# Four weight buffers parked in two row slots while the expert rows start, and another order of selection, queries and rows

## The chip, the cores and the metric

One core of a Trainium2 chip runs the whole kernel in one launch. Times are microseconds of device time; the metric is the median of the runs.

## The reference, cut to what matters

Two blocks of two layers each work on 256 tokens of 1024 features in fp32. The second block is the one that the change touches. A layer of it mixes four token mixers, projects, and then routes every token to expert rows:

```
q  = (x @ w_q)                       # 8 heads, 2 halves of 128 each
sc = q . sub_keys                    # 128 scores for each half
top 16 of each half -> 256 sums -> best 16, idx; gate = softmax(best)
act = gelu(u_tab[idx] . x)           # 16384 rows of 1024 in each table
y  += (gate * act) * v_tab[idx]      # 8 heads x 16 rows for each token
```

## The kernel before, in words

**Weights** come as a stream of chunks of 128 x 1024 fp32 (0.524 MB). SP loads chunk c into a raw buffer. ScalarE writes its high part (L1369), GpSimd (L1247) or VectorE (L2069) the low part, raw minus high; TensorE multiplies with both and adds to w_used when a chunk is used. A raw buffer is free when the low part is made, so SP waits for the low part of the buffer's chunk before. The second block has 42 chunks a layer: 18 for the mixers' input, 8 for the output projection (18 to 25), and 26 to 41 are the query weights, two for each of the 8 heads. It uses four raw buffers. The split chunks lie in w_split, six pairs; pairs 4 and 5 serve chunks 22 and 23 only, the later query chunks take pairs 0 and 1.

**Rows.** The 256 tokens are two tiles of 128. With 8 heads and 16 picks, a layer fetches 256 gathers (called rows in the code, ROWS), each one row of the joined table (2048 fp32) for each of 128 tokens, 1.049 MB. GpSimd issues them as indirect DMAs (L1331) into slots. VectorE takes the dot products of the first half of the row with x (L2419), ScalarE applies gelu and the gate and makes diagonal matrices (L1692 to L1703), TensorE multiplies these with the second half of the row and accumulates over the tile (weighted_rows). They go in batches of two; a unit is one head of one tile, 16 gathers or 8 batches. Ten slots are used up to gather 89, fifteen from 90 on. Slots 6 to 9 lie over w_split: 6 and 7 over pairs 4 and 5, 8 and 9 over pairs 2 and 3.

**Order.** Each engine works off a queue written out by hand. Gathers start while the queries of the later heads are still to be computed. VectorE picks the experts of a unit in six parts (stages), put behind dots of batches by SELECT_AT. TensorE's halves of a query and its key scores stand between batches (QUERY_AT, QUERY_LATER); GpSimd's low parts of the query chunks stand between gathers (LOWS_AT). GpSimd waits before a gather for its slot: for w_used where weights lay there, else for row_used of the slot's gather before. Since its queue has one order, whatever stands behind such a wait waits too. At a layer's end SP resets semaphores (turn) and loads the next layer's first three chunks.

## Time and profile before

| | us |
|---|---|
| median of 3 runs | 2305.95 (2296.69 to 2306.26) |
| the profiled execution's own time | 2299.8 |
| its span | 2297.7 |
| TensorE, VectorE, GpSimd, ScalarE busy | 1951.7, 1401.6, 1190.8, 950.0 |
| gathers, all 512: share of 16 DMA engines | 56.4% |

The span is that of the instructions on the one core; the execution's own time has 2.1 us more around it. The two layers of the first block end at 680, the two of the second block take 680 to 1490 and 1490 to 2298. A busy share is a mean over stages with different limits, so the stages are read one by one. Clock times in the text are us from the span's start.

### The profile page before, as it was taken

The numbers are of one execution on the slowest core, as the hardware profiler recorded it, in microseconds if no ns is written. First come the engines' busy times: TensorE is split into PE (matmuls) and PEld (weight loads), VectorE is DVE, ScalarE is ACT, GpSimd is POOL, SyncE is SP. The second block draws the span as 40 slices with busy tenths as digits, with TensorE's granted clock in tenths as the row PEclk, the third lists the DMA queues.
The fourth block names the chain that finished last, engine by engine and source line by source line (L and its number), as shares of the span: only waits on it lengthen the run. The fifth ranks groups of instructions, "written<-read, shape, count | busy, mean of one in ns | idle before, by whom it ended". The sixth has DMA issues, their size and how long they took to land.

```text
span 2297.7 us, 26964 instructions
## 1 busy us (share of the span) xinstructions
PE 1951.7 (85%) x8576; PEld 1287.0 (56%) x8576; DVE 1401.6 (61%) x3166; ACT 950.0 (41%) x2289; POOL 1190.8 (52%) x816
## 2 busy tenths in 40 slices
PE   7989998999999889987777777798899877777776
PEld 6889998789988765543223222387654422232222
DVE  6442116531127888776777665578897767776655
ACT  6644336644335534333233332356344332333322
POOL 6759868758873156645344343141466544443441
PEclk9999999999999989999999999998899999999999
DMA  5436544435545289999999999763799999999997
GB/s 180 148 114 201 184 159 161 157 112 191 183 172 210 92 327 403 421 420 421 421 421 420 422 420 421 292 221 108 294 415 421 420 421 421 421 421 422 421 421 293
DMA packets 118020, 700.27 MB, mean 305 GB/s; under 512 B 13968, under 2 KB 13968, under 8 KB 51856
## 3 DMA queue, kind: packets, MB, share of 16 engines
q0 software_dynamic: 73728, 536.90, 56.4%
q1 hardware_dynamic: 44176, 161.96, 20.3%
q8 instruction: 56, 0.92, 0.2%
q14 instruction: 60, 0.49, 0.1%
HBM read 697.76 MB, written 1.05 MB: 304 GB/s over the span
## 4 chain that ended last, share of the span: by engine, by line
PE 46%; DMA 38%; DVE 7%; ACT 4%; issue 3%; POOL 2%; DVEq 0%; SPq 0%; POOLq 0%; ACTq 0%
PE ps L648 45%; DMA late_row<-in_table,arena 18%; DMA arena<-in_table,arena 16%; DMA row_sb<-in_table,arena 3%; DVE late_row L2419 1%; POOL w_split L1247 1%; POOL arena L1331 1%; DVE arena L2419 1%; DVE arena L2083 1%; ACT diag L1703 1%; DVE w_split L2069 1%; POOL late_row L1331 1%; ACT w_split L1369 0%; ACT arena L1697 0%; ACT arena L1692 0%
## 5 line engine op out<-in xcount | busy, mean ns | idle before, releaser
L1247 POOL TENSOR_TENSOR w_split<-raw,w_split 128x1024 fp32r<-128x1024 f32 x248 | 606.0, 2468 | 329.1 <-ACT w_split L1369 326.6
L648 PE MATMUL ps<-late_row,diag 128*128 128x512 f32 x1000 | 467.6, 610 | 129.4 <-ACT diag L1703 129.4
L648 PE MATMUL ps<-hT_hi,w_split 128*128 128x256 f32 (+1 forms) x2688 | 522.3, 292 | 14.2 <-DVE hT_lo L2145 5.3
L648 PE MATMUL ps<-arena,diag 128*128 128x512 f32 x888 | 424.8, 620 | 124.3 <-ACT diag L1703 124.3
L648 PEld LDWEIGHTS ps<-hT_hi,w_split 128*128 128x128 f32 x2688 | 435.8, 196 | 26.2 <-issue 13.8
L1331 POOL DMA_INDIRECT late_row<-in_table,arena x250 | 266.5, 1066 | 322.3 <-PE ps L648 294.8
L2419 DVE CUSTOM_DVE_ANT_0 late_row<-late_row,x_res 128x1024 f32<-128x1024 f32 x250 | 317.7, 1274 | 170.1 <-DMA late_row<-in_table,arena 164.4
L1331 POOL DMA_INDIRECT arena<-in_table,arena x222 | 247.2, 1113 | 325.7 <-PE ps L648 265.6
L648 PEld LDWEIGHTS ps<-late_row,diag 128*128 128x128 f32 x1000 | 183.0, 192 | 401.7 <-ACT diag L1703 216.6
L648 PE MATMUL ps<-hT_lo,w_split 128*128 128x256 f32 (+2 forms) x1344 | 386.8, 288 | 0.0
L2419 DVE CUSTOM_DVE_ANT_0 arena<-arena,x_res 128x1024 f32<-128x1024 f32 x222 | 289.0, 1306 | 154.4 <-DMA arena<-in_table,arena 150.3
L1692 ACT ACTIVATE arena<-arena 128x2 f32<-128x2 f32 x260 | 52.6, 202 | 766.0 <-DVE arena L2419 765.7
L648 PEld LDWEIGHTS ps<-arena,diag 128*128 128x128 f32 x888 | 163.9, 194 | 363.7 <-ACT diag L1703 199.3
L1369 ACT ACTIVATE w_split<-raw 128x1024 fp32r<-128x1024 f32 x288 | 300.7, 1059 | 160.9 <-DMA raw<-in_stream 112.5
L648 PEld LDWEIGHTS ps<-hT_lo,w_split 128*128 128x128 f32 (+1 forms) x1344 | 263.9, 196 | 7.7 <-issue 5.7
L648 PE MATMUL ps<-w_split,hT_hi 128*128 128x512 f32 x640 | 204.9, 402 | 15.5 <-DVE arena L1936 3.6
L1834 DVE TENSOR_TENSOR arena<-arena,ps 128x256 f32<-128x256 f32 x44 | 18.5, 421 | 303.0 <-ACT arena L1419 303.0
L1703 ACT ACTIVATE diag<-ident,arena 128x128 f32<-128x128 f32 x512 | 174.2, 387 | 0.3
L648 PEld LDWEIGHTS ps<-w_split,hT_hi 128*128 128x128 f32 x640 | 120.4, 192 | 47.0 <-issue 9.1
L1697 ACT ACTIVATE arena<-arena 128x1 f32<-128x1 f32 x512 | 123.3, 287 | 8.5
L648 PE MATMUL ps<-w_split,hT_lo 128*128 128x512 f32 x320 | 126.7, 396 | 0.0
L648 PE MATMUL ps<-w_split,hidw_hi 128*128 128x512 f32 x352 | 109.4, 392 | 0.0
(280 smaller groups left out, 1940.1 us busy)
## 6 DMA issues: line engine op xcount, KB each, us to landing
raw<-in_stream SPq DMA_DIRECT2D x288, 512.0 KB, 3.3
row_sb<-in_row SPq DMA_DIRECT2D x2, 2306.5 KB, 10.7
late_row<-in_table,arena POOLq DMA_INDIRECT x250, 30.2
arena<-in_table,arena POOLq DMA_INDIRECT x222, 29.3
arena<-in_sub SPq DMA_DIRECT2D x2, 1024.0 KB, 10.4
arena<-in_small SPq DMA_DIRECT2D x2, 640.0 KB, 8.4
x_res<-in_x SPq DMA_DIRECT2D x1, 1024.0 KB, 5.8
out_x<-x_res SPq DMA_DIRECT2D x2, 512.0 KB, 5.2
```

The costliest lines, as they stand in the source:

```text
L648: ins = nc.tensor.matmul(o, lhsT, rhs, start=start, stop=stop)
L1247: pool.tensor_tensor(w_lo[pair], raw[:, at % raws, :], w_hi[pair].bitcast(F32), ALU.subtract).then_inc(lo_ready, 1)
L1331: pool.indirect_dma_start(out=slots[slot_of[n]], out_offset=None, in_=table, in_offset=bass.IndirectOffsetOnAxis(ap=picked[:, u, at:at + 1 ...
L1369: A(w_hi[pair_of(c, self.pairs, self.narrow)], raw[:, slot, :], ACT.Copy).then_inc(hi_ready, 1)
L1692: A(acts[:, some], dots[:, some], ACT.Gelu).then_inc(acts_ready, 1)
L1697: A(acts[:, n:n + 1], acts[:, n:n + 1], ACT.Copy, scale=gate[:, n // TOP, n % TOP:n % TOP + 1]).then_inc(acts_gated, 1)
L1703: A(diag[:, n % DIAGS, :], ident[:], ACT.Copy, scale=acts[:, n:n + 1]).then_inc(diag_ready, 1)
L1834: V.tensor_tensor(full, value, gate, ALU.mult).then_inc(gate_step, 1)
L2069: V.tensor_tensor(w_lo[pair], raw[:, c % RAW2, :], w_hi[pair].bitcast(F32), ALU.subtract).then_inc(dve_lo_ready, 1)
L2083: step(V.scalar_tensor_tensor(out=dst[:, c, :], in0=x, scalar=tap, in1=dst[:, c, :], op0=ALU.mult, op1=ALU.add))
L2419: ins = V.tensor_tensor_reduce(out=x, in0=x, in1=x_res[:, n // TILE_ROWS, :], scale=1.0, scalar=0.0, op0=ALU.mult, op1=ALU.add, accum_out= ...
```

## The change

The second block gets nine raw buffers. Five are used in turn for all chunks but four; the fifth of them is the memory of three constant tiles (rel, after, before), which the second block doesn't need once its masks are made. The other four, the parked ones, are the halves of row slots 6 and 7 and hold the query chunks 30 to 33, loaded when 24 chunks are used. Gathers 0 to 11 run on the eight other slots (FIRST_LAP); gather 12 is the first in slot 6 and 15 the first in slot 7, each after the low parts of the chunks parked there. From 16 to 89 the ten slots are used in turn, then fifteen.

The queues at the opening change: TensorE takes key scores 1 before the first batch, and puts the halves of query 2 behind batches 0 and 1. ScalarE empties query 1 before the first diagonals and query 2 before those of batch 2. GpSimd makes the low parts of head 2 before gathers 10 and 11, of head 3 before 12 and 14, of head 4 before 16 and 20. Heads 5 to 7 stay at the first and fifth gather of a unit. Selection of unit u ends behind batch 8u - 7 instead of some batches earlier, and the gates' exponential moves with it. At the end of a layer that another follows, SP waits for all dots before it loads the next layer's first chunks.

```diff
@@ -49,7 +49,8 @@
...
-RAW2, PAIR2 = 4, 4
+RAW2, PAIR2, PARKED = 5, 4, 4
+PARAMS_AT, LATE_AT = 3, 5
@@ -75,13 +76,19 @@
...
-LOWS_AT = {14: (2, 0), 15: (2, 1), 17: (3, 0), 19: (3, 1), 24: (4, 0), 28: (4, 1)}
-LOWS_AT.update({(h - HEADS_FIRST) * TOP + 4 * k: (h, k) for h in range(5, PH) for k in range(2)})
-QUERY_AT = {0: (5, 6, 7), 1: (2, 4, 6)}
-QUERY_LATER = (0, 2, 5)
-OPENING = 3
+LOWS_AT = (10, 11)
+HEAD_LOWS_AT = (12, 14)
+OPENING = 2
+RAW_HOME = ([c % RAW2 for c in range(N2_NARROW)] + [RAW2 + k for k in range(PARKED)]
+            + [c % RAW2 for c in range(N2_NARROW, N2 - PARKED)])
+NTH_RAW = [RAW_HOME[:c].count(RAW_HOME[c]) for c in range(N2)]
+RAW_BEFORE = [max((k for k in range(c) if RAW_HOME[k] == RAW_HOME[c]), default=None) for c in range(N2)]
+PARK_FREE = N2_MIX + 6
+FIRST_LAP = (0, 1, 2, 3, 4, 5, 8, 9, 0, 1, 2, 3, 6, 4, 5, 7)
+LAP = (8, 9, 0, 1, 2, 3, 6, 4, 5, 7)
...
-SELECT_AT = {0: 0, 1: 0, 2: 3, 3: 3, 4: 0, 5: 2}
+SELECT_AT = {0: 0, 1: 2, 2: 2, 3: 2}
+SELECT_AT.update({b: 1 for u in range(2, UNITS) for b in range(u * UNIT_BATCHES - 12 + (u == 2), u * UNIT_BATCHES - 6 + (u == 2))})
@@ -186,14 +193,14 @@
...
+        MASKS = 3 + 3 * AH + 4
...
-        raw = sb("raw", [P, max(RAW1, RAW2), CH])
+        raw = sb("raw", [P, RAW2 - 1, CH])
...
-        rel = sb("rel", [P, 3 * P])
-        after = sb("after", [P, 3 * P])
-        before = sb("before", [P, 3 * P])
+        distances = sb("distances", [P, 3, 3 * P])
+        rel, after, before = distances[:, 0], distances[:, 1], distances[:, 2]
@@ -229,6 +236,8 @@
...
+        raws_at = [raw[:, k, :] for k in range(RAW2 - 1)] + [distances.rearrange("p k c -> p (k c)")[:, 0:CH]]
+        raws_at += [late_row[:, 2 + k // 2, k % 2 * CH:(k % 2 + 1) * CH] for k in range(PARKED)]
@@ -368,8 +377,10 @@
...
-        assert ALL_SLOTS_FROM % QUERY_SLOTS == 0
-        slot_of = [n % QUERY_SLOTS if n < ALL_SLOTS_FROM else (n - ALL_SLOTS_FROM + QUERY_SLOTS) % SLOTS for n in range(ROWS)]
+        turned = (ALL_SLOTS_FROM - len(FIRST_LAP)) % len(LAP)
+        FULL_LAP = (*range(QUERY_SLOTS, SLOTS), *LAP[turned:], *LAP[:turned])
+        slot_of = [FIRST_LAP[n] if n < len(FIRST_LAP) else LAP[(n - len(FIRST_LAP)) % len(LAP)] if n < ALL_SLOTS_FROM
+                   else FULL_LAP[(n - ALL_SLOTS_FROM) % SLOTS] for n in range(ROWS)]
@@ -539,7 +550,7 @@
...
-                sp.dma_start(raw[:, slot, :], stream[c]).then_inc(w_ready[slot], 16)
+                sp.dma_start(raws_at[slot], stream[c]).then_inc(w_ready[slot], 16)
@@ -562,20 +573,26 @@
...
                 for c in range(EARLY, N2):
-                    if c >= RAW2:
-                        low_part_made(sp, c - RAW2)
-                    load(base + c, c % RAW2)
+                    if RAW_BEFORE[c] is not None:
+                        low_part_made(sp, RAW_BEFORE[c])
+                    if RAW_HOME[c] == RAW2:
+                        sp.wait_ge(w_used, PARK_FREE)
                     if c == RAW2 - 1:
+                        sp.wait_ge(mask_ready, MASKS)
+                    load(base + c, RAW_HOME[c])
+                    if c == PARAMS_AT:
                         for dst, src in params:
                             sp.dma_start(dst, src).then_inc(par_ready, 16)
-                    if c == RAW2 + N2 % RAW2 - 1:
+                    if c == LATE_AT:
                         for dst, src in late:
...
 
-            def turn(n, chunks, low, following):
+            def turn(n, chunks, low, following, rows=0):
 
...
                 sp.wait_ge(lo_ready, low)
+                if rows and following is not None:
+                    sp.wait_ge(dots_ready, rows)
                 sp.sem_inc(first, 1)
@@ -609,7 +626,7 @@
...
                         store_tile(t)
-                turn(l + (1 + DEPTH), N2, low_parts(N2 - 1), following)
+                turn(l + (1 + DEPTH), N2, low_parts(N2 - 1), following, BATCHES)
 
@@ -1166,26 +1182,24 @@
...
                 query(1, 1)
+                key_scores(1)
                 weighted_rows(0)
-                key_scores(1)
+                query(2, 0)
                 weighted_rows(1)
-                weighted_rows(2)
-                query(2, 0)
-                weighted_rows(3)
                 query(2, 1)
-                key_scores(2)
-
-
-                for b in range(OPENING + 1, BATCHES):
+
+
+                for b in range(OPENING, BATCHES):
                     u, at = BATCH_ROWS[b][0] // TOP, BATCH_ROWS[b][0] % TOP // BATCH
...
                     h = u + HEADS_FIRST
-                    first_half, second_half, scored_at = QUERY_AT.get(u, QUERY_LATER)
-                    if h < PH and at == first_half:
+                    if b == OPENING:
+                        key_scores(HEADS_FIRST - 1)
+                    if h < PH and at == (2 if u == 0 else 0):
                         query(h, 0)
-                    if h < PH and at == second_half:
+                    if h < PH and at == (4 if u == 0 else 2):
                         query(h, 1)
-                    if h < PH and at == scored_at:
+                    if h < PH and at == (6 if u == 0 else 5):
                         key_scores(h)
@@ -1311,17 +1325,22 @@
...
                     u, at = n // TOP, n % TOP
+                    h = u + HEADS_FIRST
+                    if h < PH and at == (HEAD_LOWS_AT[0] if u == 0 else 0):
+                        query_low_part(h, 0)
+                    if h < PH and at == (HEAD_LOWS_AT[1] if u == 0 else 4):
+                        query_low_part(h, 1)
                     if n in LOWS_AT:
-                        query_low_part(*LOWS_AT[n])
+                        query_low_part(HEADS_FIRST - 1, LOWS_AT.index(n))
                     if u == 0 and at in FIRST_PICKS:
...
                         pool.wait_ge(picks_ready, u + len(FIRST_PICKS))
-                    if n == FREE_SLOTS - 2:
-                        pool.wait_ge(w_used, N2_QUERY - 2)
-                    if n == FREE_SLOTS:
+                    if n == FIRST_LAP.index(8):
 
                         pool.wait_ge(w_used, N2_NARROW - 2)
+                    if n in (FIRST_LAP.index(6), FIRST_LAP.index(7)):
+                        low_part_made(pool, N2_NARROW + (1 if slot_of[n] == 6 else 3))
                     if n == ALL_SLOTS_FROM:
@@ -1362,11 +1381,13 @@
...
-                    slot = c % self.raws
-                    act.wait_ge(w_ready[slot], i * (16 * step // self.raws) + 16 * (c // self.raws + 1))
+                    in_block2 = self.narrow == N2_NARROW
+                    slot = RAW_HOME[c] if in_block2 else c % self.raws
+                    nth = NTH_RAW[c] if in_block2 else c // self.raws
+                    act.wait_ge(w_ready[slot], i * (16 * step // self.raws) + 16 * (nth + 1))
...
-                    A(w_hi[pair_of(c, self.pairs, self.narrow)], raw[:, slot, :], ACT.Copy).then_inc(hi_ready, 1)
+                    A(w_hi[pair_of(c, self.pairs, self.narrow)], raws_at[slot], ACT.Copy).then_inc(hi_ready, 1)
@@ -1703,34 +1724,30 @@
...
                 query_high_part(2, 0)
+                empty_query(1)
                 diags_of(0)
-                empty_query(1)
+                empty_scores(1)
+                query_high_part(2, 1)
                 diags_of(1)
-                empty_scores(1)
-                diags_of(2)
-                query_high_part(2, 1)
-                diags_of(3)
                 query_high_part(3, 0)
                 empty_query(2)
+                diags_of(2)
+                empty_scores(2)
                 query_high_part(3, 1)
-                empty_scores(2)
                 for b in range(OPENING + 1, BATCHES):
...
                         gate_exp(1)
-                    if b == UNIT_BATCHES:
-                        gate_exp(2)
-                    first_half, second_half, scored_at = QUERY_AT.get(u, QUERY_LATER)
-                    if h + 1 < PH and at == (2 if u > 1 else first_half + 1):
+                    if h + 1 < PH and at == (4 if u == 0 else 2):
                         query_high_part(h + 1, 0)
-                    if h < PH and at == (4 if u > 1 else second_half + (u == 1)):
+                    if h < PH and at == (5 if u == 0 else 4):
                         empty_query(h)
-                    if h + 1 < PH and at == (5 if u > 1 else second_half + 1):
+                    if h + 1 < PH and at == (6 if u == 0 else 5):
                         query_high_part(h + 1, 1)
-                    if 0 < u < UNITS - 2 and at == 6:
-                        gate_exp(u + 2)
+                    if 0 < u < UNITS - 1 and at == 3:
+                        gate_exp(u + 1)
                     if h < PH and at == 7:
@@ -2469,7 +2486,7 @@
...
                     dots_of(b)
-                    for _ in range(SELECT_AT.get(b, 1 if b < 2 * UNIT_BATCHES or 1 <= at <= len(stages) else 0)):
+                    for _ in range(SELECT_AT.get(b, 0)):
                         if picking:
```

Left out are the same changes of names at each use of the buffers (raws_at, RAW_HOME) and of rel, after and before.

## Rows read from the trace of the kernel before

**Rows 1.** The page: its span, the chunk's high part, the chunk loads.

```profile
span 2297.7 us, 26964 instructions
...
L1369 ACT ACTIVATE w_split<-raw 128x1024 fp32r<-128x1024 f32 x288 | 300.7, 1059 | 160.9 <-DMA raw<-in_stream 112.5
...
raw<-in_stream SPq DMA_DIRECT2D x288, 512.0 KB, 3.3
```

**Rows 2.** Windows: length, busy PE, PEld, DVE, ACT, POOL, granted clock, DMA share, GB/s.

```profile
800.00:810.00 10.00, 8.22 (x70) 7.57 (x67) 8.34 (x21) 3.14 (x9) 0.00 (x0) 1.00 0.01 2
810.00:820.00 10.00, 8.69 (x48) 8.72 (x48) 9.48 (x31) 2.33 (x3) 3.67 (x3) 0.64 0.40 132
820.00:830.00 10.00, 9.28 (x54) 8.91 (x53) 6.20 (x18) 5.11 (x9) 7.73 (x8) 0.67 1.01 418
...
890.00:900.00 10.00, 9.47 (x35) 5.27 (x35) 8.99 (x19) 3.43 (x15) 8.60 (x7) 1.00 0.91 336
```

**Rows 3.** The same view, 100 us of the steady stretch.

```profile
1150.00:1250.00 100.00, 75.23 (x158) 29.88 (x159) 72.31 (x167) 36.78 (x115) 43.54 (x40) 0.97 1.01 421
```

**Rows 4.** The same view, the second layer's opening.

```profile
1710.00:1720.00 10.00, 10.00 (x42) 5.94 (x41) 8.00 (x13) 4.23 (x14) 8.44 (x5) 1.00 1.01 397
```

**Rows 5.** SP's queue in order of time: start us, us, what, how many.

```profile
795.38 0.33 SPq L542 DMA_DIRECT2D raw<-in_stream  x1
...
818.04 1.46 SPq L542 DMA_DIRECT2D raw<-in_stream  x2
...
842.27 0.33 SPq L542 DMA_DIRECT2D raw<-in_stream  x1
...
915.62 0.33 SPq L542 DMA_DIRECT2D raw<-in_stream  x1
...
990.00 1.28 SPq L542 DMA_DIRECT2D raw<-in_stream  x3
```

**Rows 6.** The chain that ended last, at the first layer's end: start us, us, what.

```profile
1480.78 1.23 DVE late_row L2419
...
1490.53 1.28 ACT L1369
```

**Rows 7.** ScalarE in order of time, early in the mixing stage.

```profile
701.86 1.06 ACT L1369 ACTIVATE w_split<-raw 128x1024 fp32r<-128x1024 f32 x1 [1.25 <-DMA raw<-in_stream]
```

**Rows 8.** GpSimd in order of time: start us, us, engine, line.

```profile
810.86 1.13 POOL L1331 DMA_INDIRECT arena<-in_table,arena  x1 [15.50 <-DVE arena L2348]
...
832.88 0.94 POOL L1331 DMA_INDIRECT arena<-in_table,arena  x1 [3.01 <-PE ps L648]
...
839.89 2.36 POOL L1247 TENSOR_TENSOR w_split<-raw,w_split 128x1024 fp32r<-128x1024 f32 x1
...
852.58 1.67 POOL L1331 DMA_INDIRECT late_row<-in_table,arena  x1 [4.87 <-DVE arena L2397]
```

**Rows 9.** TensorE in order of time, the same columns.

```profile
830.62 3.70 PE L648 MATMUL ps<-arena,diag 128*128 128x512 f32 x8 [0.78 <-ACT diag L1703]
834.16 1.05 PE L648 MATMUL ps<-arena 128*128 128x128 f32 x8
...
842.39 0.36 PE L648 MATMUL ps<-hT_hi,w_split 128*128 128x256 f32 x1
...
845.22 0.28 PE L648 MATMUL ps<-hT_hi,w_split 128*128 128x256 f32 x1
849.13 5.40 PE L648 MATMUL ps<-late_row,diag 128*128 128x512 f32 x8 [3.63 <-ACT diag L1703]
```

**Rows 10.** ScalarE in order of time, the opening.

```profile
828.27 1.28 ACT L1692 ACT_TABLE_LOAD   x1
...
830.19 0.68 ACT L1703 ACTIVATE diag<-ident,arena 128x128 f32<-128x128 f32 x2
830.77 0.57 ACT L1664 ACTIVATE arena<-ps 128x512 f32<-128x512 f32 x1
```

**Rows 11.** TensorE in order of time, the second layer's opening.

```profile
1657.90 3.70 PE L648 MATMUL ps<-late_row,diag 128*128 128x512 f32 x8 [3.63 <-ACT diag L1703]
```

More of the change, by code:

```diff
@@ L426, in two_blocks_kernel @@
         arrived = {n: sem(f"{n}_arrived") for n in ("pe", "act", "dve", "pool")}
-        w_ready = [sem(f"w_ready{i}") for i in range(max(RAW1, RAW2))]
+        w_ready = [sem(f"w_ready{i}") for i in range(RAW2 + PARKED)]
         first = sem("layer_first")
@@ L620, in two_blocks_kernel @@
         CONSTS = 4
-        MASKS = 3 + 3 * AH + 4
         LAST_SUMS = 2 + 2 * TT + TT
@@ L1202, in _ @@
             pool.memset(ident[:], 0.0).then_inc(const_ready, 1)
-            pool.iota(rel[:], pattern=[[1, 3 * P]], base=-P, channel_multiplier=-1,
+            pool.iota(rel, pattern=[[1, 3 * P]], base=-P, channel_multiplier=-1,
                       allow_small_or_imprecise_dtypes=True).then_inc(rel_ready, 1)
@@ L1219, in second_constants @@
                 for h in range(AH):
-                    pool.tensor_scalar(window[:, h], rel[:], 2.0 ** (-2.0 * (h + 1)) * 64 ** 0.5, 0.0, ALU.mult,
+                    pool.tensor_scalar(window[:, h], rel, 2.0 ** (-2.0 * (h + 1)) * 64 ** 0.5, 0.0, ALU.mult,
                                        ALU.add).then_inc(mask_ready, 1)
@@ L1246, in low_part @@
                 pair = pair_of(at, pairs, narrow)
-                pool.tensor_tensor(w_lo[pair], raw[:, at % raws, :], w_hi[pair].bitcast(F32),
+                pool.tensor_tensor(w_lo[pair], raws_at[RAW_HOME[at] if narrow == N2_NARROW else at % raws], w_hi[pair].bitcast(F32),
                                    ALU.subtract).then_inc(lo_ready, 1)
@@ L1760, in setup @@
                 dve.wait_ge(rel_ready, 1)
-                step(V.tensor_scalar(after[:], rel[:], 0.0, None, ALU.max))
-                step(V.tensor_scalar(before[:], rel[:], -1.0, 0.0, ALU.mult, ALU.max))
+                step(V.tensor_scalar(after, rel, 0.0, None, ALU.max))
+                step(V.tensor_scalar(before, rel, -1.0, 0.0, ALU.mult, ALU.max))
                 step.settle()
-                step(V.tensor_tensor(absd[:], after[:], before[:], ALU.add))
+                step(V.tensor_tensor(absd[:], after, before, ALU.add))
                 step.settle()
@@ L2068, in low_part @@
                         dve.wait_ge(w_used, used_before(c, PAIR2, N2_NARROW))
-                    V.tensor_tensor(w_lo[pair], raw[:, c % RAW2, :], w_hi[pair].bitcast(F32),
+                    V.tensor_tensor(w_lo[pair], raws_at[RAW_HOME[c]], w_hi[pair].bitcast(F32),
                                     ALU.subtract).then_inc(dve_lo_ready, 1)
```

## The prediction

> **What bounds the kernel now.** I read four views, in this order. The page gives the span, 2297.7 us, and the forms of the weight work [rows 1]. Then the windows, because the question of this change is who supplies the DMA engines. In each of the two layers of the second block the reader should see three states: before the expert rows start the engines are nearly idle (2 GB/s at 800 to 810), from about 820 they run at 418, and from then on at 421 until the rows are through [rows 2, 3]. A gather is 128 x 8 KB = 1.049 MB, so at 421 GB/s it costs 2.49 us of DMA time, and 256 of them 638 us. That is the whole time from 820 to the last landing at 1480.8 but for what else passes through the same engines. TensorE is idle a quarter of it. So a layer of the second block is (start of the gathers) + (bytes still to move) / 421 + (DMA idle time), and nothing that happens on an engine counts unless it changes one of the three. Third, the queues of SP, GpSimd, TensorE and ScalarE at the opening, for the order in which they release each other. Last, the chain of waits at the layer's end.
>
> The exact start of the full stretch: 810 to 820 moved 1.32 MB, of which 1.05 is gather 0; the other 0.27 MB is 0.65 us, so 819.35 [rows 2]. Idle time in the present opening: 336 instead of 421 GB/s in 890 to 900 is 2.0 us, and with the small deficits of the other windows about 2.6. The second layer's only large one is 397 GB/s over 10 us, 0.6; call it 0.9 in all [rows 4].
>
> **Bytes taken out of the full stretch.** Now chunk c waits for the low part of c - 4, so SP's issues can be numbered backwards: 31 at 795.4, 32 and 33 at 818.0, and eight (34 to 41) from 842.3 to 915.6 [rows 5]. Ten chunks of 0.524 MB pass while the engines are full, 1.245 us each. After the change 30 to 33 have buffers of their own and wait only until 24 chunks are used, which is inside the output projection, shortly before 800; behind them in SP's queue 34 waits for the low part of 25, 35 and 36 for those of 26 and 27 (the latter is what released SP at 795.4). All are ready. So 30 to 36, 3.7 MB or 8.7 us, go at about 797 into a stretch that moved 2 GB/s. 37 and 38 wait for 28 and 29, as 32 and 33 do now, and go at 818; 39 to 41 later. Five chunks remain instead of ten: **-6.2 us a layer, -12.5 in all**.
>
> **The next layer's first loads.** They are issued at 990.0, three chunks amid full DMA [rows 5]. The new wait on all dots moves them to about 1482.1, when the DMA is idle: **-3.7 us**, once. SP has nothing queued behind them but the layer's turn. They are covered by the last sums and the norm: a chunk lands 3.3 us after issue [rows 1], 1485.4, and ScalarE begins the next layer at 1490.5 [rows 6]. Without that cover they would cost those 3.3 us. The last layer has no such loads.
>
> **Fifth buffer in the mixing stage.** ScalarE waited 1.25 us for a chunk at 701.9, on the path [rows 7]; I found no other such wait on the chain. It can be worth 0 to 1.25 us a layer; I take **-1** for both. The wait on the masks is met before the layer opens. The five parts of selection that move to later batches lie on VectorE, which waits for rows; the last part of unit u runs behind the dots of batch 8u - 7, its first row needs slot space from batch 8u - 5 on ten slots. Nothing.
>
> **The opening, where the cost is.** Gathers 0 to 7 are issued as now, from 810.9 on [rows 8]. Then today gathers 8 and 9 have slots too, 10 to 13 follow the first two batches of weighted rows, and no query stands between these batches; gather 16 goes at 852.6. After the change gather 8 needs gather 0's slot, and the queues interlock: the low part of head 2 stands in GpSimd's queue in front of gather 10, and the first half of query 2 stands in TensorE's in front of batch 1, which frees gather 10's slot. I walk it with durations of the rows: a batch 3.7 us, its first gather's slot handed to GpSimd 2.26 after its start (830.62 to 832.88), half a query 3.1 (842.4 to 845.5), key scores 1.05, low part 2.4, emptying a bank 0.6, high part 1.06, a table load 1.28, from its end to the first diagonal 1.07 [rows 1, 8 to 10].
> - Query 1 ends at 829.84 (0.78 before 830.62). ScalarE empties it first, 830.45, then loads the table and makes the diagonals, 832.8. Batch 0 starts 2.2 later than now: gathers 8 and 9 at 835.1 and 836.9.
> - Low part (2,0) 837.9 to 840.3; half query to 843.5; batch 1; gather 10 at 845.8. Low part (2,1) to 849.4; gather 11 at 849.6.
> - Half query (2,1) to 852.6, and low part (3,0) before gather 12, 853.9. ScalarE has emptying query 2 in front of batch 2's diagonals: 854.3; gather 13 at 856.5, batch 2 ends 858.0.
> - Key scores 2 to 859.05, emptied 859.65, high part (3,1) 860.7, low part 863.2: gather 14 at 863.3, 15 at 865.3.
> - Gather 16 stands behind low part (4,0), whose high part ScalarE makes after batch 4's diagonals. These come after batch 3's (1.5), the gate's exponential (a table load and 0.4) and a second table load: 866.6; high part 867.6, low part 870.1, **gather 16 at 870.2** against 852.6 now.
>
> Its data flow from about 871.5 (an issue takes 1.1 to 1.8 on GpSimd [rows 8]). Between 819.35 and 871.5 the DMA then has gathers 1 to 15 (37.4 us) and chunks 37 and 38 (2.5): 39.9 of 52.1 us. **12.2 us idle a layer**, 24.4 in all, for the present 2.6 + 0.9: **+20.9**. From gather 17 on GpSimd issues faster than 2.49 us again and ten slots are enough, as now.
>
> TensorE's clock: after 3.6 us of waiting the batch at 849.1 took 5.4 us, not 3.7; the same batch of the second layer, after the same wait, took 3.7 [rows 9, 11]; and the window at 810 to 820 had a mean granted clock of 0.64, between the two levels of 1.2 and 2.4 GHz [rows 2]. The new opening has a wait of 3.9 us (836.5 to 840.4) and several of 2. With three waits to meet it I take one such slowdown a layer, 1.7: **+3.4**.
>
> **Sum.** -12.5 - 3.7 - 1 + 20.9 + 3.4 = **+7**. Against the profiled execution's own 2299.8 that is 2307; that execution is 6 below the median of 2306 (2297 to 2306). I forecast **2313 us**. About 0.5%, 11.5 us, is what a measurement can tell from no change.
>
> **Rivals.**
> 1. The supply holds, faster. Place: gathers 8 to 16. If queries and batches overlapped better than my walk, only the two missing slots would count, 5 us of DMA time a layer: 10 - 3.5 - 12.5 - 3.7 - 1 = -11, 2295. For it: landing times in full stretches leave some gathers queued. Against: each step of the walk is a wait in a queue with one order. It decides if gather 16 goes before about 863; at 10 us idle a layer the change is even.
> 2. TensorE falls to the lower clock for most of the opening, slower. Two half queries and three batches on the walk's path at 1.5 to 1.7 more each are 8 us a layer, where I took 1.7: 13 more, 2326. For it: the slow batch above came after one such wait and the opening makes three. Against: in the steady stretch, with TensorE idle a quarter of the time in short pieces, the clock was 0.97 [rows 3]. The Trainium skill, TensorE: Matmul & The Clock Gate (Part 1: The HAM clock gate), says that throttled is the default state and only activity releases it; by that rule each long wait starts the next piece slow, which is this rival; the trace shows it for one such wait of two.
> 3. The change does not take bytes out, because PARK_FREE or the order in SP's queue holds the parked loads until 818: the 6.2 a layer are gone, 2325. The window at 800 to 810 speaks against it.
> 4. The moved first loads are not covered: +3.3, inside the range.
>
> **Chances.** The walk as it stands (2303 to 2321) 0.50; rival 1 0.20; rival 2 0.22; rival 3 and the rest 0.08. The range from rival 1 to rival 2 is 2295 to 2328. Of the first case about a seventh lies above 2317.5, and a small part of rival 1 within 0.5%: faster 0.17, same 0.48, slower 0.35.
>
> **What would show it.** SP's seven issues at about 797 and a DMA share near 0.9 at 797 to 806; two issues at 818; no load at 990 but three at 1482. Gather 8 at 835, gather 10 at 846, gather 14 at 863, gather 16 at 870; DMA windows well below 421 between 845 and 871, none below after 880. GpSimd's wait before gather 10 ended by TensorE, TensorE's before query 2 by GpSimd. The prediction is wrong if the windows from 845 to 870 stay near 421, or if the stream after 880 shows new gaps.

## The result, and the profile after

The changed kernel took 2317.15 us (median of 7 runs, 2311.73 to 2320.37), the kernel before 2303.98 on the same chip (7 runs, 2296.69 to 2306.26). The ratio is 1.0055, interval 1.0041 to 1.0068: slower by 13 us. The forecast was 2313, which was +7 on the median of 2306 that the kernel before then had. The profiled execution of the changed kernel took 2317.15 as well, with a span of 2315.2; that of the kernel before (2299.8) lies below its median, so between the two traces the spans differ by 17.5 us.

**What came as forecast.** SP's queue in order of time, in the first layer's opening (start us, us, what, how many). It answers to [rows 5]:

```profile
800.06 1.75 SPq L553 DMA_DIRECT2D late_row<-in_stream  x4
801.85 1.46 SPq L553 DMA_DIRECT2D raw<-in_stream  x3
...
820.31 0.33 SPq L553 DMA_DIRECT2D raw<-in_stream  x1
821.45 0.33 SPq L553 DMA_DIRECT2D distances<-in_stream  x1
...
1489.66 1.28 SPq L553 DMA_DIRECT2D raw<-in_stream  x3
```

The four parked chunks go into the row slots, three more into raw buffers behind them, all seven between 800.06 and 803.4; two more follow once the first gathers are out, and nothing goes at 990, for the next layer's first loads now stand at the layer's end. The whole trace is 2.3 us late here (gather 0 at 813.13 in the place of 810.86) because the first block took so much longer in this execution; that stretch moves by chance (below), so what follows counts from gather 0.

Windows of the first opening (length, busy PE, PEld, DVE, ACT, POOL, granted clock, DMA share, GB/s). They answer to [rows 2]:

```profile
800.00:810.00 10.00, 8.93 (x70) 8.25 (x68) 8.94 (x18) 1.94 (x5) 0.00 (x0) 1.00 0.90 339
...
830.00:840.00 10.00, 8.12 (x34) 4.88 (x32) 6.41 (x23) 6.26 (x15) 0.81 (x1) 0.83 1.02 425
840.00:850.00 10.00, 5.53 (x28) 4.80 (x27) 9.40 (x23) 0.00 (x0) 4.17 (x3) 0.83 0.72 280
850.00:860.00 10.00, 7.66 (x32) 5.43 (x30) 5.59 (x9) 1.10 (x2) 8.06 (x5) 0.83 0.60 206
860.00:870.00 10.00, 8.49 (x43) 5.96 (x44) 4.26 (x13) 5.53 (x14) 3.86 (x3) 1.00 0.64 215
870.00:880.00 10.00, 9.55 (x40) 5.63 (x39) 5.41 (x15) 5.67 (x17) 7.95 (x7) 1.00 0.71 265
880.00:890.00 10.00, 10.00 (x30) 4.88 (x29) 8.96 (x21) 5.08 (x18) 8.11 (x7) 1.00 1.01 419
```

The engines that moved 2 GB/s at 800 to 810 now move 339, and the price is the hole from 840 to 880: 280, 206, 215, 265. The same four windows of the kernel before had nearly the full stream:

```profile
840.00:850.00 10.00, 6.37 (x33) 4.23 (x32) 9.61 (x23) 1.35 (x6) 7.36 (x4) 1.00 1.01 417
850.00:860.00 10.00, 8.52 (x39) 5.52 (x37) 8.94 (x13) 2.93 (x4) 6.00 (x3) 0.83 1.02 421
860.00:870.00 10.00, 8.79 (x20) 4.13 (x21) 9.46 (x30) 6.83 (x20) 4.96 (x3) 0.83 1.02 419
870.00:880.00 10.00, 8.92 (x54) 6.79 (x53) 9.64 (x20) 2.08 (x5) 6.75 (x6) 1.00 1.01 415
```

As idle DMA time I count each 5 us window's missing share of 421 GB/s, from 15 to 130 us after gather 0; windows above 421 count against it. It is 17.1 us in the first layer and 14.6 in the second. The kernel before had 2.6 and 0.9.

**Why the hole is there.** GpSimd in order of time (start us, us, engine, line, what, idle before and its releaser). It answers to [rows 8]:

```profile
839.20 0.94 POOL L1350 DMA_INDIRECT arena<-in_table,arena  x1 [10.37 <-PE ps L664]
840.79 1.68 POOL L1350 DMA_INDIRECT arena<-in_table,arena  x1 [0.66 <-PE ps L664]
842.49 2.36 POOL L1261 TENSOR_TENSOR w_split<-late_row,w_split 128x1024 fp32r<-128x1024 f32 x1
851.59 1.14 POOL L1350 DMA_INDIRECT arena<-in_table,arena  x1 [6.74 <-PE ps L664]
852.75 2.50 POOL L1261 TENSOR_TENSOR w_split<-late_row,w_split 128x1024 fp32r<-128x1024 f32 x1
855.40 0.96 POOL L1350 DMA_INDIRECT arena<-in_table,arena  x1 [0.15 <-issue]
856.38 2.38 POOL L1261 TENSOR_TENSOR w_split<-late_row,w_split 128x1024 fp32r<-128x1024 f32 x1
858.92 1.76 POOL L1350 DMA_INDIRECT late_row<-in_table,arena  x1 [0.16 <-POOL w_split L1261]
863.77 0.94 POOL L1350 DMA_INDIRECT arena<-in_table,arena  x1 [3.09 <-PE ps L664]
867.76 2.38 POOL L1261 TENSOR_TENSOR w_split<-late_row,w_split 128x1024 fp32r<-128x1024 f32 x1 [3.06 <-ACT w_split L1390]
870.28 1.76 POOL L1350 DMA_INDIRECT row_sb<-in_table,arena  x1
...
876.62 0.95 POOL L1350 DMA_INDIRECT late_row<-in_table,arena  x1
```

and TensorE, the same columns, which answers to [rows 9]:

```profile
835.12 5.40 PE L664 MATMUL ps<-arena,diag 128*128 128x512 f32 x8 [1.10 <-ACT diag L1724]
844.99 0.35 PE L664 MATMUL ps<-hT_hi,w_split 128*128 128x256 f32 x1 [4.47 <-POOL w_split L1261]
...
849.30 0.29 PE L664 MATMUL ps<-hT_hi,w_split 128*128 128x256 f32 x1
849.43 3.60 PE L664 MATMUL ps<-arena,diag 128*128 128x512 f32 x8
855.30 0.39 PE L664 MATMUL ps<-hT_hi,w_split 128*128 128x256 f32 x1 [2.27 <-POOL w_split L1261]
```

Read the two together, by the names behind the arrows. Gather 8 waited 10.37 us for TensorE's batch 0. Only behind gathers 8 and 9 does GpSimd take off the low part of query (2,0), at 842.49. TensorE waited 4.47 us for that low part, worked half a query, and then batch 1. Gather 10 waited 6.74 us for batch 1. It is the interlock of the prediction, link by link, with both engines waiting in turn: TensorE has 5.53 of 10 us in the window from 840. Against the walk, counted from gather 0:

| us after gather 0 | gather 8 | 10 | 12 | 13 | 14 | 16 |
|---|---|---|---|---|---|---|
| predicted | 24.2 | 34.9 | 43.0 | 45.6 | 52.4 | 59.3 |
| first layer | 26.1 | 38.5 | 45.8 | 50.6 | 57.1 | 63.5 |
| second layer | 23.2 | 35.3 | 43.1 | 47.7 | 54.2 | 60.5 |

In the kernel before gather 8 went at 16.0, 10 at 22.0, 14 at 31.5 and 16 at 41.7.

### The profile page after: what moved, and what is told of

It is laid out like the page before. It is cut to its first block, busy times and chain, and to the rows that moved or that the text cites. A ratio compares the mean times of both kernels' runs of the same rounds, so it can differ in the third digit from the quotient of the medians.

```text
span 2315.2 us, 27031 instructions
## 1 busy us (share of the span) xinstructions
PE 1958.5 (85%) x8576; PEld 1292.2 (56%) x8576; DVE 1394.4 (60%) x3166; ACT 947.1 (41%) x2287; POOL 1196.2 (52%) x816
## 4 chain that ended last, share of the span: by engine, by line
PE 46%; DMA 38%; DVE 6%; ACT 4%; POOL 4%; issue 4%; DVEq 0%; ACTq 0%; POOLq 0%; SPq 0%
PE ps L664 44%; DMA arena<-in_table,arena 21%; DMA late_row<-in_table,arena 16%; POOL w_split L1261 2%; DMA row_sb<-in_table,arena 1%; POOL arena L1350 1%; DVE arena L2436 1%; DVE arena L2100 1%; DVE late_row L2436 1%; DVE w_split L2086 1%; ACT diag L1724 1%; POOL late_row L1350 0%; ACT w_split L1390 0%; PE ps L696 0%; ACT hT_hi L1413 0%
## 5 line engine op out<-in xcount | busy, mean ns | idle before, releaser
L1261 POOL TENSOR_TENSOR w_split<-raw,w_split 128x1024 fp32r<-128x1024 f32 x236 | 577.2, 2470 | 328.6 <-ACT w_split L1390 328.0
L2436 DVE CUSTOM_DVE_ANT_0 late_row<-late_row,x_res 128x1024 f32<-128x1024 f32 x246 | 310.2, 1263 | 180.1 <-DMA late_row<-in_table,arena 174.1
L1390 ACT ACTIVATE w_split<-raw 128x1024 fp32r<-128x1024 f32 x266 | 278.2, 1058 | 122.0 <-DMA raw<-in_stream 112.4
L664 PE MATMUL ps<-row_sb,diag 128*128 128x512 f32 x160 | 81.4, 633 | 33.9 <-ACT diag L1724 33.9
```

Of the source, the lines that this page charges most:

```text
L664: ins = nc.tensor.matmul(o, lhsT, rhs, start=start, stop=stop)
L1261: pool.tensor_tensor(w_lo[pair], raws_at[RAW_HOME[at] if narrow == N2_NARROW else at % raws], w_hi[pair].bitcast(F32), ALU.subtract).then_ ...
L1390: A(w_hi[pair_of(c, self.pairs, self.narrow)], raws_at[slot], ACT.Copy).then_inc(hi_ready, 1)
L2436: ins = V.tensor_tensor_reduce(out=x, in0=x, in1=x_res[:, n // TILE_ROWS, :], scale=1.0, scalar=0.0, op0=ALU.mult, op1=ALU.add, accum_out= ...
```

## The experiments

All ratios are to the kernel before, with runs of it on the same chip; the intervals are of 95%. The plain quotient of the two medians differs from the ratio by up to 0.0012 (2.8 us). "Idle" is the DMA idle time of the two openings, summed as above; the kernel before has 3.5 us in both together, the changed one 31.7.

**The moved first loads, taken back.** The changed kernel without the turn's wait for the dots:

```
-turn(l + (1 + DEPTH), N2, low_parts(N2 - 1), following, BATCHES)
+turn(l + (1 + DEPTH), N2, low_parts(N2 - 1), following)
```

> The changed kernel, but SP does not wait for the dots before it loads the next layer's first three chunks. Theory (the opening's queues starve the DMA, the moved loads are a gain): the three loads go back to about 993, amid full DMA, the first layer's rows end 3.7 us later, time about 4 us above the changed kernel, 2320 to 2322 (ratio to the kernel before 1.007). Rival (the moved loads are not covered at the layer's turn and are part of the loss): time 3 us below the changed kernel, 2314.

Measured: 2320.7 us, ratio 1.0071 (1.0054 to 1.0089), 0.0016 or 3.7 us above the changed kernel's, the size of the term; but the two intervals overlap.

**The buffers with the order of before.** The changed kernel's nine buffers and moved loads, with before's order of queries, batches and selection; the low parts of head 2 stand at rows 10 and 12, since the parked slots must be emptied:

```
-LOWS_AT = (10, 11)
-OPENING = 2
+LOWS_AT = {10: (2, 0), 12: (2, 1), 17: (3, 0), ...}
+OPENING = 3
...
-FIRST_LAP = (0, 1, 2, 3, 4, 5, 8, 9, 0, 1, 2, 3, 6, 4, 5, 7)
+FIRST_LAP = (0, 1, 2, 3, 4, 5, 8, 9, 0, 1, 2, 3, 6, 4, 5, 8, 9, 0, 1, 7)
```

> The changed kernel's nine buffers and its moved loads, with the order of queries, batches, empties and selection of the kernel before; the low parts of head 2 stand before gathers 10 and 12, slot 6 starts with gather 12, slot 7 with gather 19. Theory (the interlock of low part, query and batch is the loss, not the buffers): idle DMA time at the opening falls from 17 and 15 us to 2 to 5 a layer, gather 16 is issued about 853 to 857, time 2291 to 2297 (ratio 0.995 to 0.997). Rival (two slots fewer are the loss, whatever the order): idle stays at 10 or more a layer, time 2305 or above.

Measured: 2300.52 us, 0.9983 (0.9968 to 0.9998), idle 11.7. The loss is gone while the buffers stay, so it lies in the new order (of queries, batches, low parts and selection taken together); a small gain over before is left, smaller than expected.

**Eight slots alone.** Before, with rows on eight slots until row 12 and nothing else:

```
-slot_of = [n % QUERY_SLOTS if n < ALL_SLOTS_FROM else ...]
+FIRST_LAP = (0, 1, 2, 3, 4, 5, 8, 9, 0, 1, 2, 3, 6, 4, 5, 7)
```

> The kernel before, whose gathers use slots 6 and 7 only from gathers 12 and 15 on, in the changed kernel's order of slots; nothing else is changed. Theory: gathers 8 to 11 follow the first two batches as their slots come free, the DMA stays fed, at most 2 us a layer, ratio 1.000 to 1.002. Rival (the missing slots are the loss): 5 us or more a layer, ratio 1.004 or above.

Measured: 0.9996 (0.9982 to 1.0011), idle 3.9. Gather 8 goes at 23.1 in the place of 16.0, gather 12 at 29.9 in the place of 26.4, and the stream shows no hole: the eight gathers already issued are 20 us of data. Two slots fewer cost nothing that the times show.

**The moved loads alone.** Before, with the turn's new wait.

> The kernel before with one part of the change alone: SP waits for all dots before the next layer's first three loads. Theory: 3.7 us less, ratio 0.998 to 0.999, loads landed before ScalarE asks for them. Rival (not covered): ratio 1.000 to 1.002, with ScalarE's first high part of the next layer waiting for a DMA.

Measured: 0.9988 (0.9974 to 1.0003). Both the expected -3.7 us and no change at all lie inside the interval, so it decides nothing.

**The low parts of head 2 sooner.** The changed kernel with one line edited:

```
-LOWS_AT = (10, 11)
+LOWS_AT = (8, 9)
```

> The changed kernel with the low parts of head 2 in front of gathers 8 and 9 instead of 10 and 11; nothing else. Theory (the interlock): the half queries 2 no longer wait for GpSimd, batches 1 and 2 start 4 to 6 us earlier, gather 16 is issued about 56 us after gather 0 instead of 60.5 to 63.5, idle falls by 4 to 6 us a layer, time 8 to 12 below the changed kernel: 2305 to 2310, ratio 1.000 to 1.003. Rival (two slots fewer, or the clock, is the loss and the position of two subtractions is not): 2315 to 2319.

Measured: 2290.57 us, 0.9936 (0.9912 to 0.9961), from 4 runs; idle 11.6; gather 16 at 51.8. The direction was right and the size far more than expected. The profiled execution is the slowest of the four (2299.63), 9 us above their median, so its trace can show only a part of that size. GpSimd and TensorE of this kernel:

```profile
831.17 2.93 POOL L1261 TENSOR_TENSOR w_split<-late_row,w_split 128x1024 fp32r<-128x1024 f32 x1 [1.97 <-ACT w_split L1390]
838.45 0.95 POOL L1350 DMA_INDIRECT arena<-in_table,arena  x1 [4.34 <-PE ps L664]
839.42 2.40 POOL L1261 TENSOR_TENSOR w_split<-late_row,w_split 128x1024 fp32r<-128x1024 f32 x1
841.98 0.96 POOL L1350 DMA_INDIRECT arena<-in_table,arena  x1 [0.16 <-issue]
844.25 1.29 POOL L1350 DMA_INDIRECT arena<-in_table,arena  x1 [1.31 <-PE ps L664]
```

```profile
835.69 3.70 PE L664 MATMUL ps<-arena,diag 128*128 128x512 f32 x8 [1.10 <-ACT diag L1724]
838.83 0.68 PE L664 MATMUL ps<-hT_hi,w_split 128*128 128x256 f32 x1
...
842.10 3.60 PE L664 MATMUL ps<-arena,diag 128*128 128x512 f32 x8
845.13 0.68 PE L664 MATMUL ps<-hT_hi,w_split 128*128 128x256 f32 x1
```

The first subtraction now lies in the 10 us in which GpSimd waited for batch 0 anyway. TensorE goes from batch 0 to the half query to batch 1 with no wait between them, and from 830 on its granted clock is 1.00: half a query takes 3.3 us (838.83 to the batch at 842.10), not 4.4. The windows:

```profile
840.00:850.00 10.00, 8.56 (x51) 6.44 (x50) 9.47 (x17) 2.43 (x7) 7.93 (x6) 1.00 1.02 420
850.00:860.00 10.00, 9.86 (x46) 6.53 (x47) 9.79 (x16) 5.54 (x13) 5.12 (x4) 1.00 0.77 307
860.00:870.00 10.00, 9.55 (x40) 5.64 (x39) 9.69 (x27) 5.66 (x19) 8.68 (x6) 1.00 0.83 297
```

**Batch 1 ahead of query (2,0).** In the changed kernel, on TensorE:

```
-query(2, 0)
 weighted_rows(1)
+query(2, 0)
```

> The changed kernel with batch 1 in front of both halves of query 2 on TensorE; nothing else. Theory (all later links of the chain bind until gather 16): gathers 10 and 11 go some 5 us sooner, but batch 2 still stands behind query 2, so gather 16 and with it the idle sum change by at most 2 us a layer: ratio 1.003 to 1.006. Rival (the loss is the late freeing of the slots of gathers 10 and 11): idle falls by 5 us or more a layer, ratio 1.001 or below.

Measured: 0.9983 (0.9969 to 0.9998), idle 20.1, gather 16 at 55.4. My expectation failed and the rival held. Turning two queue entries on TensorE breaks the ring as well: gather 10 goes at 31.9 (38.5 in the changed kernel), gather 11 at 35.5 (42.3), and the later links do not take it back.

**The new selection plan alone.** In the order of before, with the new places of the gates' exponentials that go with it:

```
-SELECT_AT = {0: 0, 1: 0, 2: 3, 3: 3, 4: 0, 5: 2}
+SELECT_AT = {0: 0, 1: 2, 2: 2, 3: 2}
+SELECT_AT.update({b: 1 for u in range(2, UNITS) for b in range(...)})
```

> The kernel before with the changed plan of selection and of the gates' exponentials alone. Theory: no cost and no gain, ratio 0.999 to 1.001, DMA windows after the opening stay at 421. Rival (selection by need comes too late for a unit's first gathers): GpSimd waits on VectorE before the first gather of the units, gaps below 421 in the stream, ratio 1.002 or above.

Measured: 2308.44 us, 1.0022 (1.0008 to 1.0036): about 5 us slower (3 by the medians), idle 8.4, gather 14 at 37.1 after gather 0 (31.5 before). The prediction had put this part at nothing. Its own rival, that GpSimd waits for VectorE at the first gather of a unit, is not what happened: GpSimd waits for TensorE at gather 14, and the idle time of the opening is the whole loss. VectorE and GpSimd of this kernel:

```profile
832.46 0.49 DVE L2305 MAX8 arena<-arena 128x8 f32<-128x128 f32 x2 [1.84 <-ACT arena L1669]
...
837.08 3.35 DVE L2418 CUSTOM_DVE_ANT_0 row_sb<-row_sb,x_res 128x1024 f32<-128x1024 f32 x1
```

```profile
836.65 2.71 POOL L1248 TENSOR_TENSOR w_split<-raw,w_split 128x1024 fp32r<-128x1024 f32 x1
845.59 1.21 POOL L1332 DMA_INDIRECT arena<-in_table,arena  x1 [6.24 <-PE ps L649]
```

The two stages behind batch 1 stand in VectorE's queue ahead of the dots of batch 2, and they wait for ScalarE to empty key scores 1. The second dot of batch 2 so begins 2.9 us later after gather 0 than before (28.6 for 25.7), and it takes 3.35 us in the place of 1.22, as GpSimd subtracts at that moment: 5.0 us together. In the second layer the wait for the key scores is 4.41 us and gather 14 is 7 us late.

**Two parked chunks.** The order of before and the moved loads, with chunks 30 and 31 parked in slot 6 only, so that rows have nine slots until row 12:

```
-RAW2, PAIR2, PARKED = 5, 4, 4
+RAW2, PAIR2, PARKED = 5, 4, 2
```

> The order of the kernel before and the moved loads, five buffers and only chunks 30 and 31 parked, in slot 6; slot 7 takes rows from the start, so nine slots until gather 12. Theory: three chunks leave the full stretch instead of five (-3.7 us a layer), idle falls from the 5 and 7 of the run with four parked to 1 to 3, time 2292 to 2297, at or a little below that run. Rival (the bytes moved out are what counts, the ninth slot not): 3 to 5 us above that run.

Measured: 2293.35 us, 0.9951 (0.9934 to 0.9969), idle 6.9, 7 us below the same order with four parked, which ran on another chip; the intervals just overlap. The row stages of the two are alike (table below), so these 7 us are in no part that the edit explains.

**One low part sooner.** The changed kernel with `LOWS_AT = (8, 11)`.

> Both subtractions of the third head ahead of gathers 8 and 9 made the changed kernel 27 us faster, against the 8 to 12 that I had set down. This one puts only the first of them ahead of gather 8 and leaves the second ahead of gather 11, to see which link of the chain the time hung on. Theory: TensorE gets its half query right behind batch 0 at the full clock (batch 0 and batch 1 at 3.6 to 3.7 us, no half query at 4.6), gathers 8 to 10 go as in the run with both sooner (24.8, 28.3 less the 2.5 us subtraction, and about 30 us after gather 0), and the second subtraction holds the second half query back by some 4 us, so that gather 16 goes at 55 to 56 us after gather 0 (51.8 with both, 63.5 and 60.5 with none) and the idle DMA time is 8 to 10 us a layer (5.8 with both, 17.1 and 14.6 with none): ratio to the kernel before 0.996 to 0.998, so the first subtraction carries some two thirds of the 27 us. Rival: the second one carries as much, since TensorE stands idle ahead of the second half query and works it and the batch behind it at half clock (4.6 and 5.4 us): gather 16 at 58 us or later and a ratio of 1.000 to 1.003.

Measured: 2304.98 us, 1.0009 (0.9996 to 1.0021), idle 16.8, gather 16 at 53.8. The gathers and the idle time are those of the theory (gather 16 even somewhat sooner), the ratio is the rival's; its row stages are 1.6 us shorter than before's, and its mixing stages, 131.7 and 133.1 us, the longest of all. GpSimd of this kernel (gathers 10, 11 and 12 are its gathers here):

```profile
847.82 0.94 POOL L1350 DMA_INDIRECT arena<-in_table,arena  x1 [3.61 <-PE ps L664]
848.78 2.35 POOL L1261 TENSOR_TENSOR w_split<-late_row,w_split 128x1024 fp32r<-128x1024 f32 x1
851.29 0.96 POOL L1350 DMA_INDIRECT arena<-in_table,arena  x1 [0.16 <-issue]
852.27 2.73 POOL L1261 TENSOR_TENSOR w_split<-late_row,w_split 128x1024 fp32r<-128x1024 f32 x1
855.15 1.76 POOL L1350 DMA_INDIRECT late_row<-in_table,arena  x1 [0.15 <-POOL w_split L1261]
```

The first low part gave back about half of the idle time (31.7 to 16.8) and 15.4 of the 19.4 us that both gave in the row stages. The first two batches take 3.7 and 3.6 us, and the second half query, after a wait of 1.92 us, runs at the full clock, so the rival had the ratio but not its reason. The second low part still holds gathers 11 and 12 back while GpSimd works two subtractions with only gather 11 between them.

**Three variants of the run with both low parts sooner.** Nine slots (`PARKED = 2`); the second low part of head 3 ahead of gather 15 (`HEAD_LOWS_AT = (12, 15)`, 14 before); and before's selection plan (SELECT_AT and its default turned back; the gates' exponentials keep their new places).

> The run with both subtractions sooner, with five raw buffers and only chunks 30 and 31 parked (nine row slots until row 12). Theory of the prediction: two chunks a layer go back into the stretch in which the DMA is full, 1.25 us each, +5 us over both layers, and the idle time falls from 5.8 us a layer to about 3, -6 us: within 2 us of the run with both sooner, ratio 0.993 to 0.994. Rival: as between the two runs in the order of before (four parked 0.9983, two parked 0.9951), the ninth slot is worth 7 us more than the bytes cost: ratio near 0.990. Second rival: idle is bound by TensorE's chain, not by slots, and stays at 5 us a layer, so the bytes cost their 5 us: ratio 0.996.

> The run with both subtractions sooner, with the second subtraction of the fourth head ahead of gather 15 in the place of gather 14 (gather 15 needs it anyway, for it takes the slot of the parked chunk). In the run with both sooner gather 14 waited behind it until 858.92, while its own slot had been free since about 854. Theory: gather 14 goes 4 to 5 us sooner (at 40 us after gather 0 in the place of 45), the idle time falls by 2 to 3 us a layer and the ratio by 0.002, to 0.991 to 0.992. Rival: gather 14 takes DMA time that the gathers behind it lack in any case, or the subtraction itself comes 1 us later for it and the half query too: ratio as before, 0.9935 to 0.995.

> The run with both subtractions sooner, with the selection spread of the kernel before (0, 0, 3, 3, 0, 2 stages in the first batches and one in most later ones) and the new places of the gates' exponentials. In the order of before the new spread cost 5 us (ratio 1.0022), with gather 14 at 37 to 39 us after gather 0 against 31.5. Theory: the new spread holds VectorE with two stages in batches 1 to 3 just where rows are waited for, whatever the order of the queries, so taking it back gives 3 to 5 us: ratio 0.991 to 0.992. Rival: in the new order batches 1 and 2 wait for half queries anyway, so the stages stand beside idle time: ratio as with both sooner, 0.9935 to 0.995, or worse where the three stages in batches 2 and 3 hold the dot products.

Measured: 0.9968 (0.9955 to 0.9981), 0.9967 (0.9954 to 0.9979) and 0.9969 (0.9955 to 0.9983), 12 runs each; idle 10.4, 12.2 and 15.0. None beat the run that they started from. In the second, gather 14 went at 40.4 in the place of 45.2, and gather 16 at 51.6 against 51.8, so the data behind it came no sooner: the rival. In the third, gather 8 is 1.4 us later and the next ones up to 2.3. The plan of before gives no gain in this order, although it was the better one in its own. In the changed kernel's trace the two stages wait only 0.46 us for the key scores, which TensorE there computes ahead of batch 0, and batch 2 stands behind both half queries anyway.

**All of them in one table.** "Whole" is the measured ratio as us. "Rows" is read from the profiled executions: from gather 0 to the first table load of the next layer, plus from the second layer's gather 0 to the end, against the 679.7 + 678.1 us of before. The last column is worked out: the idle time over before's 3.5, less 6.2 us a layer for the chunks out of the full stream (7.5 in all where two are parked in the place of four), less 3.7 for the moved loads, each only where the kernel has that part.

| kernel | idle, us | ratio | whole | rows | account |
|---|---|---|---|---|---|
| changed | 31.7 | 1.0055 | +13 | +13.8 | +12 |
| loads back | 29.6 | 1.0071 | +16 | +14.8 | +14 |
| order of before | 11.7 | 0.9983 | -4 | -6.2 | -8 |
| eight slots alone | 3.9 | 0.9996 | -1 | +2.0 | 0 |
| moved loads alone | 5.1 | 0.9988 | -3 | -1.2 | -2 |
| both low parts sooner | 11.6 | 0.9936 | -15 | -5.6 | -8 |
| batch 1 first | 20.1 | 0.9983 | -4 | +2.0 | 0 |
| selection alone | 8.4 | 1.0022 | +5 | +5.3 | +5 |
| two parked | 6.9 | 0.9951 | -11 | -6.0 | -8 |
| one low part sooner | 16.8 | 1.0009 | +2 | -1.6 | -3 |
| nine slots, both sooner | 10.4 | 0.9968 | -7 | -3.2 | -4 |
| gather 14 sooner | 12.2 | 0.9967 | -8 | -3.5 | -7.5 |
| before's selection, both sooner | 15.0 | 0.9969 | -7 | -1.8 | -5 |

Rows and account agree within 4.0 us in all thirteen, and in twelve within 2.9. All thirteen are on the same side: the rows are longer than the account, by 1.8 us in the mean, and what that is was not looked for. The account is close to an identity (a stage that DMA bounds lasts its bytes over the rate plus the idle time), so it says where the time went; why the DMA was idle is shown by the runs that move one thing. The whole times stray further, for two stretches that no edit aims at move from one execution to the next. In the same profiles the first block ends between 681.1 and 686.0 us, and the mixing stage (a layer's first table load to gather 0) takes 127.3 to 133.1 us, in kernels with four raw buffers and with five. So of the 27 us between the changed kernel and the one with both low parts sooner, the traces show 19.4 in the row stages (13.8 + 5.6). The rest is not explained by the edit; that run has only 4 executions, and its three variants with 12 stand at 0.9967 to 0.9969.

The best versions are both low parts sooner, 0.9936 (0.9912 to 0.9961), and two parked chunks in before's order, 0.9951 (0.9934 to 0.9969). Both beat the kernel before and the changed one. In the row stages they and the four parked chunks in before's order are within 0.6 us of each other; which is the best is open.

## Why the prediction came out as it did

**The mechanism held.** The order of the walk, who waits for whom at gathers 8, 10, 13 and 14, the hole in the windows and the full stream after 880 are all in the trace. Undoing the order removed the loss with the buffers kept, the slots by themselves cost nothing, and breaking one link of the ring in either of its queues (GpSimd's or TensorE's) took the kernel to or below the time of before. The sign was right, and 2317.15 is in the range; the sum was 6 us short, +7 against +13 by the medians, and 10 short by the two traces (17.5). At 0.55% the change lies just above the 0.5% that was taken as measurable, to which only a chance of 0.35 had been given.

**Bytes, -12.5.** Seven loads at 800 to 803 and two at 820 to 822, as written, and 339 GB/s at 800 to 810. No run has this term by itself, but the two pairs with four and two parked chunks test its price of 1.25 us. In before's order two parked chunks have 4.8 us less idle time and by the price 5.0 more of bytes, so +0.2, and the row stages differ by 0.2. In the order with both low parts sooner they have 1.2 less and 5.0 more, +3.8; the row stages grew by 2.4.

**Moved loads, -3.7, once.** 3.7 us by the ratios of the first run and the changed kernel, 3 by that of the run alone (1 by its medians); neither can be told from zero by itself. The trace of the first run has row stages only 1.0 us longer than the changed kernel's, with 2.1 less idle time, which makes 3.1. A term of this size is at the edge of what can be read. The cover held: they go at 1489.66, and ScalarE begins the next layer with a table load at 1497.99, so they have 8.3 us where 3.3 was counted with.

**Fifth buffer, -1: nothing that shows.** The wait of [rows 7] is still there, 1.12 us, and in the second layer two larger ones have come, of 1.51 and 2.37. ScalarE:

```profile
704.11 1.06 ACT L1390 ACTIVATE w_split<-raw 128x1024 fp32r<-128x1024 f32 x1 [1.12 <-DMA raw<-in_stream]
...
1511.01 1.06 ACT L1390 ACTIVATE w_split<-distances 128x1024 fp32r<-128x1024 f32 x1 [1.51 <-DMA distances<-in_stream]
...
1517.62 1.06 ACT L1390 ACTIVATE w_split<-raw 128x1024 fp32r<-128x1024 f32 x1 [2.37 <-DMA raw<-in_stream]
```

The two mixing stages took 128.7 and 130.5 us here, 128.9 and 129.1 before: +1.3 in the place of -1, all inside the 127.3 to 133.1 of the other kernels.

**Idle time, +20.9, mis-sized.** It was predicted at 12.2 us a layer and is 17.1 and 14.6, so +28.2. Two steps of the walk were too short. First, pieces on it ran wholly or in part at the lower clock. In the first layer these are batch 0 (5.4 us for 3.7) and both half queries of head 2 (4.4 us, from 844.99 to 849.43, and 4.6, for 3.1): 1.7, 1.3 and 1.5 more. Against the walk gather 8 is 1.9 us late, gather 10 3.6 and gather 13 5.0. In the second layer batch 0 took its 3.7 us, but the half queries took 5.3 and 4.6; query 1 had ended 1.5 us sooner after gather 0, so gather 8 is 1.0 early there and gather 13 2.1 late. Second, the hole is larger than the lateness of gather 16: with the walk's own count (data from 1.3 us after gather 16) the measured gathers give 16.4 and 13.4 us, and the windows 17.1 and 14.6. The window just behind gather 16 is still at 395 GB/s (878.13 to 883.13), and the one in the second layer at 339 (1690.3 to 1695.3).

**Clock, +3.4, too small and counted apart.** I took one slow piece a layer as 1.7 us beside the idle time. The slow pieces stand on the chain that releases gathers, so their price is already in the measured idle time: 4.5 us of slow pieces in the first layer and 3.6 in the second. The two terms were +24.3 together, where the idle time measured is +28.2. With this term left out, and the idle time as measured, the sum is -12.5 - 3.7 + 28.2 = +12 for the row stages, where the trace has +13.8. The whole span grew by 17.5: these 13.8, 1.3 in the mixing stages and 2.4 in the first block; the medians, in which such stretches weigh less, by 13. Rival 2, TensorE slow through most of the opening, was right in part: granted clock 0.83 in three windows, three slow pieces on the chain of the first layer and two in the second, but some 4 us a layer and not the 8.

The rule weighed there, from the Trainium skill, TensorE: Matmul & The Clock Gate (Part 1: The HAM clock gate), that throttled is the default state and activity releases it, agrees with the direction: waits and a lower clock went together, and in the run whose batches and half query follow each other without a wait the clock stayed at 1.00 from 830 on. The runs do not tell which piece pays. Batch 0 took 5.40 us in the first layer and 3.70 in the second after the same wait of 1.10 us, and the half query behind it paid in both; in the run with one low part sooner the second half query waited 1.92 us and did not pay.

**Selection, 0, wrong in the order of before.** The plan alone cost 5 us there. The step that failed took it that the five moved parts lie on VectorE in time that waits for rows anyway. There two of them stood ahead of the dots of batch 2 and waited for key scores that were not there yet, so that gather 14 came 5 us later in the first layer and 7 in the second. In the new order taking the plan back gave nothing, so for the changed kernel the term stands at zero as far as the runs can tell.

## What to carry over

Where two engines release each other through in-order queues, write both queues side by side and look for work that sits behind a wait although its own inputs are ready; here one subtraction standing two gathers too late in GpSimd's queue was most of a 13 us loss (1.0055 to 1.0009), and moving two of them, or their counterpart in the other queue, cured it. Sum the idle time of the limiting resource in windows: with the bytes it gave the length of the row stages of thirteen kernels within 4 us. Two slots fewer cost nothing here, where the gathers already issued (20 us of data) covered the wait for the next slot to come free.

## What the runs showed of the hardware that I had not expected

TensorE's clock did not fall at the end of a wait but at one place or another behind it. After 4.47 us of waiting the half query at 844.99 began at the full rate (0.40 us for two 128x256 matmuls) and fell to 0.63 us for two at 846.10. The same half query of the second layer, after 3.75 us, was slow from its first matmuls on, and took 5.3 us to batch 1 at 1661.69. Between equal sequences batch 0 and this half query thus cost 1.7 + 1.3 us more in one layer and 2.1 in the other; the second half query cost 1.5 in both. What decides which matmul is hit was not tried.

VectorE's dot products stood still while GpSimd subtracted. A dot of 128x1024 takes 1.22 us; in the trace of the kernel before 18 of them took 2.0 to 4.1 us, and each of the 18 overlaps one of GpSimd's low parts. The one in the selection run shows how: it began at 837.08, the subtraction ended at 839.36, and the dot ended at 840.43, about as long behind that as a whole dot takes. A low part on GpSimd so has a price on VectorE too; the walk had none for it, and no run here has it by itself.

Stretches that no edit touches moved by more than the effect of most edits: the first block by 4.9 us (681.1 to 686.0), the mixing stage by 5.8 us. That is the reason for counting within a stage, from gather 0, and for trusting differences of stages in two traces only beside the medians of many runs.
